# DeltaNet steps: values and normed output turned by VectorE in 32x32 blocks and through memory in place of TensorE, sums of squares by ScalarE

## The reference

```python
    qkv = jax.nn.silu(causal_conv(jnp.concatenate([dq, dk, dv], axis=-1), conv_w))
    ...
    dq = l2norm(dq.reshape(B, S, DN_HEADS, DN_DK).astype(f32)) * (DN_DK ** -0.5)
    ...
    rhs = jnp.concatenate([v * beta[..., None], k_beta * jnp.exp(gc)[..., None]], axis=-1)
    sol = lax.linalg.triangular_solve(a, rhs, left_side=True, lower=True)
    ...
    def step(state, inp):
        q_n, k_n, u_n, w_n, attn_n, gl = inp
        v_new = u_n - jnp.einsum('bhcd,bhde->bhce', w_n, state)
        o = jnp.einsum('bhcd,bhde->bhce', q_n, state) + jnp.einsum('bhcj,bhje->bhce', attn_n, v_new)
        state = state * jnp.exp(gl)[..., None, None] + jnp.einsum('bhcd,bhce->bhde', k_n, v_new)
        return state, o
    ...
    o_d = o_d * lax.rsqrt(jnp.mean(o_d * o_d, axis=-1, keepdims=True) + EPS) * dn_g.astype(f32)
    o_d = o_d.reshape(B, S, DN_V_W).astype(x.dtype) * jax.nn.silu(dz)
```

## Time and profile before

| | before |
|---|---|
| median of 3 runs | 2643.95 us (2643.94 to 2645.25) |
| span of the profiled execution | 2644.2 us |
| PE busy | 2620.6 us (99%) |
| PEld busy | 2238.1 us (85%) |
| DVE busy | 1761.1 us (67%) |
| ACT busy | 704.5 us (27%) |
| POOL busy | 798.6 us (30%) |
| granted TensorE clock | 0.999 |

### The profile page before, as it was taken

One profiled execution on the slowest core, in us unless ns is written; L12 is line 12 of the kernel. 1 busy time (PEld: TensorE's weight loads), 2 busy tenths in 40 slices (PEclk: granted clock), 3 DMA queues, 4 the chain that ended last, 5 costly groups with the idle time before them and its releaser, 6 DMA issues.

```text
span 2644.2 us, 40210 instructions
## 1 busy us (share of the span) xinstructions
PE 2620.6 (99%) x14874; PEld 2238.1 (85%) x14874; DVE 1761.1 (67%) x3972; ACT 704.5 (27%) x1440; POOL 798.6 (30%) x451
## 2 busy tenths in 40 slices
PE   8999999999999999999999999999999999999998
PEld 6888888888888899888877888888888998898887
DVE  7878777877755555434577778777877555653333
ACT  5333333333311212200143333333332221231001
POOL 3123333333312212334512233332322122132453
PEclk9999999999999999999999999999999999999999
DMA  5321222122211112433533222222222111133344
GB/s 174 100 85 58 81 69 85 53 86 65 85 50 43 41 35 76 130 96 120 157 90 88 77 74 69 73 77 72 67 77 73 43 51 43 41 106 100 99 135 152
DMA packets 293416, 217.79 MB, mean 82 GB/s; under 512 B 31747, under 2 KB 246101, under 8 KB 292965
## 3 DMA queue, kind: packets, MB, share of 16 engines
q1 hardware_dynamic: 259620, 159.07, 20.9%
q10 hardware_dynamic: 33600, 56.15, 6.3%
HBM read 176.30 MB, written 38.86 MB: 81 GB/s over the span
## 4 chain that ended last, share of the span: by engine, by line
PE 92%; DVE 3%; DMA 2%; issue 1%; ACT 1%; SPq 0%; POOL 0%; ACTq 0%; DVEq 0%; POOLq 0%
PE dense_ps L866 23%; PE dense_ps L870 23%; PE dense_ps L868 23%; PE work L849 3%; PE dense_ps L890 2%; PE dense_ps L891 2%; PE dense_ps L892 2%; PE work L1145 1%; PE work L1182 1%; PE work L1202 1%; PE work L1121 1%; PE work L1104 1%; PE work L1171 1%; PE work L1195 1%; PE work L1156 1%
## 5 line engine op out<-in xcount | busy, mean ns | idle before, releaser
L866 PE MATMUL dense_ps<-act_hi,w_hi 128*128 128x512 f32 x2552 | 1048.3, 411 | 1.7 <-DVE w_lo L1797 0.8
L870 PE MATMUL dense_ps<-act_hi,w_lo 128*128 128x512 f32 x2552 | 998.4, 391 | 0.0
L868 PE MATMUL dense_ps<-act_lo,w_hi 128*128 128x512 f32 x2552 | 997.3, 391 | 0.0
L2579 POOL TENSOR_TENSOR w_lo<-w_raw,w_hi 128x1024 fp32r<-128x1024 f32 x162 | 400.1, 2470 | 1024.5 <-ACT w_hi L1429 582.7
L870 PEld LDWEIGHTS dense_ps<-act_hi,w_lo 128*128 128x128 f32 x2552 | 479.0, 188 | 105.8
L866 PEld LDWEIGHTS dense_ps<-act_hi,w_hi 128*128 128x128 f32 x2552 | 481.0, 188 | 86.9 <-POOL act_lo L2600 2.3
L868 PEld LDWEIGHTS dense_ps<-act_lo,w_hi 128*128 128x128 f32 x2552 | 481.5, 189 | 78.8 <-issue 0.5
L1973 DVE SCALAR_TENSOR_TENSOR arena<-arena,cols 128x512 f32<-128x512 f32 x288 | 244.3, 848 | 6.1
L1429 ACT ACTIVATE w_hi<-w_raw 128x1024 fp32r<-128x1024 f32 x94 | 99.1, 1054 | 330.5 <-PE dense_ps L870 310.5
L1419 ACT ACTIVATE arena<-dense_ps 128x512 f32<-128x512 f32 x96 | 57.2, 596 | 258.5 <-PE dense_ps L870 258.5
L849 PE MATMUL work<-mk,arena 128*128 128x128 f32 x768 | 112.1, 275 | 7.9 <-DMA arena<-in_x 7.9
(11 more groups left out here) (262 smaller groups left out, 4094.7 us busy)
## 6 DMA issues: line engine op xcount, KB each, us to landing
w_raw<-in_w_in SPq DMA_DIRECT2D x138, 512.0 KB, 3.8
arena<-l_scratch SPq DMA_DIRECT2D x64, 256.0 KB
arena<-gate_scratch ACTq DMA_DIRECT2D x64, 256.0 KB, 2.7
gate_scratch<-arena ACTq DMA_DIRECT2D x36, 256.0 KB, 2.0
w_raw<-in_w_out SPq DMA_DIRECT2D x18, 512.0 KB, 3.7
o_scratch<-arena ACTq DMA_DIRECT2D x32, 256.0 KB, 2.2
w_raw<-in_w_up_dn SPq DMA_DIRECT2D x16, 512.0 KB, 3.6
arena<-o_scratch ACTq DMA_DIRECT2D x32, 256.0 KB, 3.7
```

Source lines behind the costliest of these rows:

```text
L866: eng.matmul(dense_ps[:, to, :], w_hi[:, slot, k, :], hi[:, k, seg], start=(k == 0), stop=False)
L868: eng.matmul(dense_ps[:, to, :], w_hi[:, slot, k, :], lo[:, k, seg], start=False, stop=False)
L870: mm = eng.matmul(dense_ps[:, to, :], w_lo[:, slot, k, :], hi[:, k, seg], start=False, stop=(k == KT - 1))
L2579: eng.tensor_tensor(w_lo[:, slot, :, :], w_from[second][:, :, :], w_hi[:, slot, :, :].bitcast(F32), ALU.subtract)\
```

## The change

In `even` and `odd` units PE no longer turns anything for `vt` and `ob`. In their place DVE does a `transpose` of 128x512 elements in 32x32 blocks, once of `on` (`turn_o`, slot 15, in front of `diag`) and once of the value chunks (`turn_v`, slot 16, behind `keys`), into a buffer `turned`. ACT stores that buffer to memory with four DMAs, one for each group of 32 partitions (`put`, slot 17), 128 bytes in a piece. When these have landed, ACT issues one DMA that reads the blocks back in the other order, 512 bytes in a piece (`get`, slot 20). DVE's `ob` and `vt` products move to slot 23, first `ob`, then `vt`, and take their input from the buffer `tokens` in place of PSUM. The DMA `store` moves to slot 23 on ACT. The first and the last two units of a layer keep PE's turns.

In all units the squares of q and of the output are taken by ACT chunk by chunk with an accumulated sum (`accum_out`), and DVE's two sums go.

```diff
+BACK = 2
+BACK_O, BACK_V = range(BACK)
...
-        if kind.endswith("last"):
-            at(16, "ob")
-        at(18, "store")
+        at(16 if kind.endswith("last") else 23, "ob")
+        at(18 if kind.endswith("last") else 23, "store")
...
-        at(vt, "vt")
+        at(23 if kind in ("even", "odd") else vt, "vt")
...
-        begin(15, 1, ("ob",))
+        begin(15, 1, ("turn_o",))
+        at(16, "turn_v")
+        at(17, "put")
+        at(20, "get")
...
+        turned = arena[:, swap_at:swap_at + BACK * HALF].rearrange("p (m s) -> p m s", s=32)
+        tokens = arena[:, swap_at + BACK * HALF:swap_at + 2 * BACK * HALF].rearrange("p (x c t) -> p x c t", x=BACK, c=CPH)
...
+        back_dram = nc.dram_tensor("back_scratch", [CPH * CPH * BACK, 32, P], F32)
...
 # TensorE
                         elif what == "vt":
+                            if kind in ("even", "odd"):
+                                continue
...
                         elif what == "ob":
-                            eng.wait_ge(on_ok.sem, on_ok.after(t, 1))
-                            turn(1 + b, [on[:, c, :] for c in range(CPH)]).then_inc(ob_ps.sem, 1)
+                            if kind in ("even", "odd"):
+                                continue
+                            eng.wait_ge(on_ok.sem, on_ok.after(t, 3))
+                            turn(1 + b, [on[:, c, :] for c in range(CPH)]).then_inc(back_ps.sem, 1)
...
 # ScalarE
-                            eng.activation(sq, wk[1 + nb][:, :], ACT.Square).then_inc(sq_ok.sem, 1)
+                            eng.wait_ge(qe_s.sem, qe_s.after(tn, 0))
+                            for c in range(CPH):
+                                ins = eng.activation(sq[:, c * P:(c + 1) * P], wk[1 + nb][:, c * P:(c + 1) * P], ACT.Square,
+                                                     accum_out=qss[:, c:c + 1])
+                            ins.then_inc(sq_ok.sem, 1)
...
+                        elif what == "put":
+                            u = back(l, h, b)
+                            eng.wait_ge(on_ok.sem, on_ok.after(t, 3))
+                            eng.wait_ge(back_in.sem, back_in.after(u, 0))
+                            for i in range(CPH):
+                                rows = slice(32 * i, 32 * i + 32)
+                                eng.dma_start(back_dram[:, :, rows].rearrange("m r s -> r m s"), turned[rows, :, :])\
+                                   .then_inc(back_st.sem, 16)
+                        elif what == "get":
+                            u = back(l, h, b)
+                            eng.wait_ge(back_st.sem, back_st.after(u, 64))
+                            eng.wait_ge(vb_ok.sem, vb_ok.after(tn, 0))
+                            eng.wait_ge(kd_ok.sem, kd_ok.after(tn, 1))
+                            eng.wait_ge(ob_ok.sem, ob_ok.after(t, 0))
+                            eng.dma_start(tokens.rearrange("p x c t -> p (x c) t"),
+                                          back_dram[:, :, :].rearrange("(m j) r d -> (j r) m d", j=CPH)).then_inc(back_in.sem, 16)
...
 # VectorE
+                            if step[1] and t is not None:
+                                eng.wait_ge(on_ok.sem, on_ok.after(t, 2))
...
-                            eng.tensor_reduce(qss, sq.rearrange("p (c t) -> p c t", c=CPH), mybir.AxisListType.X, ALU.add)\
-                               .then_inc(qe_s.sem, 1)
...
                         elif what == "vt":
-                            eng.wait_ge(vt_ps.sem, vt_ps.after(tn, 1))
+                            if kind in ("even", "odd"):
+                                eng.wait_ge(back_in.sem, back_in.after(back(l, h, b), 16))
+                                src = tokens[:, BACK_V]
...
-                            eng.tensor_reduce(og[:, 0, :], osq.rearrange("p (c t) -> p c t", c=CPH), mybir.AxisListType.X,
-                                              ALU.add).then_inc(og_s.sem, 1)
...
+                        elif what == "turn_o":
+                            eng.wait_ge(on_ok.sem, on_ok.after(t, 1))
+                            eng.transpose(turned_of(BACK_O), on.rearrange("p c t -> p (c t)")).then_inc(on_ok.sem, 1)
+                        elif what == "turn_v":
+                            eng.wait_ge(kqv_ok.sem, kqv_ok.after(hn, 5 + nb))
+                            eng.transpose(turned_of(BACK_V), kqv[:, 2, nb * HALF:(nb + 1) * HALF]).then_inc(on_ok.sem, 1)
                         elif what == "ob":
                             seg = slice(b * HALF, (b + 1) * HALF)
-                            eng.wait_ge(ob_ps.sem, ob_ps.after(t, 1))
-                            eng.scalar_tensor_tensor(out=sz[:, seg], in0=wk[1 + b][:, :], scalar=dngh[:, 0:1], in1=sz[:, seg],
+                            if kind in ("even", "odd"):
+                                eng.wait_ge(back_in.sem, back_in.after(back(l, h, b), 16))
+                                src = tokens[:, BACK_O].rearrange("p c t -> p (c t)")
...
+                            eng.scalar_tensor_tensor(out=sz[:, seg], in0=src, scalar=dngh[:, 0:1], in1=sz[:, seg],
                                                      op0=ALU.mult, op1=ALU.mult).then_inc(ob_ok.sem, 1)
```

51 lines of the change are left out of this document (34 added, 17 removed).

## The result

The changed kernel takes 2691.7 us (median of 4 runs, 2689.3 to 2694.2; once more, unaltered, on another occasion: 2691.1). The kernel before took 2643.9 us beside it: ratio 1.0179, interval 1.0165 to 1.0194. So it is 47.8 us slower, on the side forecast (28 us slower) and inside the range, but 20 us above the predicted time. The profiled execution took 2689.8 us, span 2688.0, which is 43.8 us more than the span before.

The account below looks back on a forecast made before the run. The prediction took PE, busy 2620.6 of 2644.2 us, as the bound: 24.6 us saved on transposes against 52.9 us of new waits, 28.3 us more, so 2672 us, range 2637 to 2735.

Parts of the forecast that it names:

- PE's saving: PE's stream: each group of four transposes removed gives back 0.44 us, 56 groups, 24.6 us in all.
- the fourth rival: PE's stream hides the transposes, so removing them gives nothing and only waits are left: 2697 us, chance 0.03.
- The turn: DVE's 128x512 transpose: 0.7 us taken, 1.2 us as upper end from four small turns.
- The wait behind `even`: Border after an `even` unit: DVE's queue makes `vt` late, PE waits 2.75 us, 14 times.
- already 0.9 us behind PE: End of the `even` unit before the change: DVE's last silu lets the first `ks` product follow 0.9 us behind PE.
- The stores: ACT's four stores, 4096 pieces: 6.25 us from first issue to last landing, ends 4.1 and 11.5 us.
- the wait behind `odd`: Border after an `odd` unit: only the transfers count, PE waits 1.0 us, 14 times.
- rival 3: Faster: stores take 4.1 to 5 us, no wait behind `odd`, 1.4 us behind `even`: 2639 us, chance 0.16.
- The sign of being wrong at 7 us: The forecast is wrong if the last store lands more than 7 us behind the first issue.
- Rival 2: Stores bound both borders: 2811 us if they take 11.5 us, 2713 us at 8 us; chance 0.20.
- ACT at 0: ACT's queue: `get` holding it and the squares in four parts cost 0; up to 1 us if cover is gone.
- 14 x (2.75 + 1.0) = 52.9 us: Sum of PE's waits behind `even` and `odd` units over 14 borders of each kind.

Follow-up runs that it names:

- the kernel without transfers: The changed kernel with stores and load left out, `ob` and `vt` reading the turned tiles directly at the unit's end: 2657.2 us, ratio 1.0048.

## Why the prediction was right in its sign and short by 20 us

- **PE's saving**: 0.44 us a group forecast, 0.42 measured (the kernel without transfers). Right; the fourth rival, that the stream hides the transposes, is out.
- **The turn**: 0.69 to 0.71 us, as taken. The upper end, by the small turns and by the Trainium skill's figure, did not come: the Trainium skill ("VectorE: DVE Perf Modes", "The three transpose paths") has 311 ns for 128x128 in bf16, and here 128x512 in f32 took 694 ns, not four times that.
- **The wait behind `even`**: 2.75 forecast, 2.19 measured, for the reason given. The copy is held by PE, `turn_v` ends 6.25 us behind its start (6.23 by the forecast), and `ob` and `vt` take 2.0 us from the last silu on. The step that was mis-sized is the untouched stretch between: from the z product to the last silu DVE took 10.70 us before, less 0.60 for `vt` makes 10.10, and it took 9.49 (317.76 to 327.25). The tap at 309.59 had lasted 1.61 us before; it lasts 1.02 now (319.93). POOL's weight split ran until 310.92 before and until 320.67 now, and both taps end just behind it: DVE comes to it later and is held shorter. The Trainium skill ("SBUF — State Buffer", "Who interferes with whom") says that a VectorE instruction with two SBUF inputs contends with a GpSimd instruction that reads SBUF, that one with at most one SBUF input does not unless it runs in a two-port mode, and that whoever issues first then blocks the other for the whole instruction. These rows agree, the `ob` of 2.65 us with its two SBUF inputs most of all: the four products L2238 with one input in PSUM start beside the same split at 318.90 and take 1.11 us, as before. One reading of the prediction was too large, without a place in the sum: that DVE is "already 0.9 us behind PE" at this border. The product can only start some 0.5 us behind PE's `ks` (329.82 - 329.30 with DVE idle), so DVE's own lag before was under 0.4 us.
- **The stores**: 6.25 us forecast from first issue to last landing, 4.4 in the steady heads, 7.6 to 7.9 behind the first two `odd` units. That pieces are paid by the piece did not hold: half of them took 1.0 us less. The load 3.8, measured 4.1. The forecast let the load go when the last store has landed; in the steady heads it goes 1.2 us after that, since it stands behind a tanh that waits for DVE, whose first tap in this stretch is held by POOL's split (1.85 us at 364.89). So the wait behind `odd`, 1.03 us forecast and 0.93 measured as a mean of 14, is near by luck: two of above 3 us come from slow stores, and twelve of about 0.55 from stores 1.9 us faster than forecast and a hold that was not in the forecast. By the trace the twelve would be nothing if the load went at 4.4 us, as rival 3 has it for fast stores; no run has the load ahead of that tanh. Why the first heads' stores are slower the runs don't tell. The sign of being wrong at 7 us was met in these two units of 28. Rival 2 (both borders bound by stores) is out: without transfers the even wait stays as it is.
- **ACT at 0**: the squares, yes. `get` costs what the tanh ahead of it holds it. `store` costs 0.27 us at ten odd borders while PE waits for `vt`, which comes 0.7 us behind `ob` and so gives ACT a start; but once `vt` stands ahead of `ob`, 1.4 to 1.5 us a head come out. I had put the copy of `v_new` "about 0.1 us" behind; I had not counted what is queued between `store` and it, 2 us.
- **The term that was missing: the clock.** The sum had -24.6 + 52.9 = 28.3. Measured, -23.5 (56 x 0.42) + 30.7 (even) + 13.0 (odd) = 20.2, 8 us less than forecast. To it come 18.7 us of half clock, which stood nowhere in the prediction, and about 4 us of new waits in the last but one unit of each layer (L1187 for the state, L1211 for ACT's copy), less 4 us of waits at the start of layer 2 that are gone. That makes 39 of the 43.8 us. Some 2.5 us more are small waits, most of them 0.27 us for ACT's copy behind an odd border; the last 2 us I can't place. So the forecast's nearness hid two errors of opposite sign.

The step that fell short is "14 x (2.75 + 1.0) = 52.9 us": it priced a wait at its length. In this kernel, whose PE is otherwise hardly ever idle, a pause of more than 2 us also cost, in part of the cases, 1.7 us of clock.

## What to carry to other kernels

Taking work out of PE's stream pays only if what replaces it doesn't stand at the end of another engine's queue. Find the place where that engine has idle time (slot 7 here) and put the work there before the kernel is timed. When an engine issues a transfer, look at both sides of it in that engine's queue. What stands ahead can hold the transfer although its data are ready (the tanh ahead of the load), and what stands behind is held while it waits (the copy of `v_new` behind `store`). Ask on which engine the next wait will come out when the first is gone; here `ob`, `vt` and `store` took turns. A transfer's start minus the first store is not the time of the stores: read their landing. And keep PE's pauses short: in these runs several of 1.5 us cost less than fewer of 2.2 with about the same sum.

## What the runs showed of the hardware

- The granted clock halved (2.4 to 1.2 GHz) at some of PE's pauses of 2.15 us and above, for 3.4 us (1.7 us lost), in other places in two executions of the same kernel, and never at pauses of 1.4 to 1.5 us. In six traces of twelve it also halved with no pause, behind 1.95 us of 16 matmuls of 16 columns and eight of 128. In the changed kernel 8 and 9 of 14 even borders have it, without transfers 3 of 14 at a length of 2.15 us; that difference stays open.
- A store of 1024 pieces of 128 bytes took 0.63 us of ACT's queue in the median to issue, up to 2.15, and landed in 2.7 us. Four of them in a row had landed 4.4 us behind the first issue in the median (7.9 at most), and four of 512 pieces 3.4 us:

```profile
L1654 ACTq DMA_DIRECT2D back_scratch<-arena x112: 319/630/2151, 130.3 to 2057.4; - x112
...
DMA to landing us min/median/max: 2.1/2.7/6.2
```

- Two DVE operations of 128x512 with all their tensors in SBUF were held when they started beside POOL's weight split (2.4 us), until it ended: `ob` took 2.65 us in place of 0.75, the first tap of a convolution 1.02 to 1.85 in place of 0.48. Operations beside the same split with an input in PSUM took their usual time (L2238, 0.33 us each), and so did the 32x128 turns (0.30 us).
